# Hybrid decoder step on one core: new shares for the decode tokens' side chain

## The reference, cut to what matters

```
x += W_out( sigmoid(g_a) * P_a(SSD(xn)) + sigmoid(g_b) * P_b(DSA(xn)) ),  xn = RMSNorm(x)
x += PEER(RMSNorm(x))
```

```
ik_past = cik[page_table].reshape(bsz, past, IDX_DIM)
score = indexer_scores(iq, concatenate([ik_past, ik]), iw)      # 4097 scores per sample
_, idx = lax.top_k(score, 256)
... gather those 256 rows of cache_k and cache_v, softmax attention
```

## Time and profile before

| | us |
|---|---|
| median of 3 runs | 5932.22 (5928.28 to 5935.11) |
| the profiled execution's own time | 5921.76 |
| its span, first to last instruction | 5920.0 |
| PE busy | 4190.6 (71%) |
| DVE busy | 3636.4 (61%) |
| POOL busy | 2584.6 (44%) |
| DMA, mean over the span | 251 GB/s |

### The profile page before, as it was taken

The page is one execution under the profiler, slowest core; times in us unless marked ns, Lnnn a source line. Parts: engine busy times, 40 slices in busy tenths (PEclk is TensorE's granted clock), DMA queues, the critical chain, the costliest instruction groups (busy, mean ns, idle before and its releaser), DMA issues. The chain is left out here.

```text
span 5920.0 us, 49064 instructions
## 1 busy us (share of the span) xinstructions
PE 4190.6 (71%) x15564; PEld 2567.8 (43%) x15564; DVE 3636.4 (61%) x7802; ACT 1156.4 (20%) x2892; POOL 2584.6 (44%) x2215
## 2 busy tenths in 40 slices
PE   6956981578677887379677777668677897265666
PEld 5334871443333665153335664453333675022222
DVE  4055528766677557576766768765668556845554
ACT  2042320111322111120422221111232211011011
POOL 0000010247555444336555443246545445477776
PEclk9975995788788998689888898879788998678788
DMA  4311740569777887579889975569777889599999
GB/s 131 115 56 54 243 132 0 178 238 322 253 256 257 315 286 269 193 271 381 304 276 328 387 260 167 188 213 338 252 258 258 281 306 311 217 343 349 347 357 342
DMA packets 579367, 1484.59 MB, mean 251 GB/s; under 512 B 60088, under 2 KB 251160, under 8 KB 572600
## 3 DMA queue, kind: packets, MB, share of 16 engines
q0 software_dynamic: 307200, 1115.82, 53.6%
q1 hardware_dynamic: 258952, 331.39, 16.8%
q10 hardware_dynamic: 12960, 34.26, 1.5%
HBM read 1435.37 MB, written 45.93 MB: 250 GB/s over the span
## 5 line engine op out<-in xcount | busy, mean ns | idle before, releaser
L2640 PE MATMUL duo<-vring,diag 128*128 128x512 f32 (+1 forms) x2544 | 1403.4, 697 | 626.4 <-DMA vring<-in_peer_v,eidx 365.7
L2526 POOL DMA_INDIRECT uring<-in_peer_u,eidx x1024 | 1248.8, 1219 | 1180.9 <-DVE uring L2558 707.6
L2593 POOL DMA_INDIRECT vring<-in_peer_v,eidx x1024 | 1158.3, 1131 | 1150.9 <-PE duo L2640 540.0
L2558 DVE SCALAR_TENSOR_TENSOR uring<-uring,xr 128x1024 f32<-128x1024 f32 x1040 | 1252.7, 1221 | 268.6 <-DMA uring<-in_peer_u,eidx 224.5
L2640 PEld LDWEIGHTS duo<-vring,diag 128*128 128x128 f32 (+1 forms) x2544 | 522.7, 219 | 1364.2 <-issue 1190.5
L2673 DVE SCALAR_TENSOR_TENSOR x_tok<-vring,wt,x_tok 128x1024 f32<-128x1024 f32 x404 | 522.1, 1292 | 379.0 <-DMA vring<-in_peer_v,eidx 352.5
L637 PE MATMUL duo<-wt,xT 128*128 128x512 f32 (+3 forms) x1440 | 607.5, 581 | 89.7 <-DMA wt<-in_w_in 89.7
L637 PEld LDWEIGHTS duo<-wt,xT 128*128 128x128 f32 (+1 forms) x1440 | 241.9, 179 | 444.8 <-issue 351.7
L2621 ACT ACTIVATE diag<-ident,wt 128x128 f32<-128x128 f32 x620 | 235.3, 397 | 1011.0 <-PE duo L2640 819.5
L492 PE MATMUL duo<-xT,wx 128*128 128x264 f32 (+1 forms) x1536 | 376.7, 409 | 37.9 <-DMA wx<-in_w_in 37.7
L492 PEld LDWEIGHTS duo<-xT,wx 128*128 128x128 f32 x1536 | 311.2, 205 | 92.8 <-DMA wx<-in_w_in 38.1
(11 more groups left out here) (462 smaller groups left out, 5076.1 us busy)
## 6 DMA issues: line engine op xcount, KB each, us to landing
wt<-in_w_in SPq DMA_DIRECT2D x32, 2048.0 KB
wx<-in_w_in SPq DMA_DIRECT2D x48, 1024.0 KB
wm<-in_w_in SPq DMA_DIRECT2D x32, 1024.0 KB
wm<-in_w_branch_a SPq DMA_DIRECT2D x32, 1024.0 KB
wq<-in_peer_wq SPq DMA_DIRECT2D x32, 1024.0 KB
tokm<-tout ACTq DMA_DIRECT2D x64, 256.0 KB
eb<-decays SPq DMA_DIRECT2D x32, 512.0 KB
s_h<-in_state_ssm SPq DMA_DIRECT2D x16, 1024.0 KB
```

Source lines behind the costliest of these rows:

```text
L2526: pool.indirect_dma_start(out=E.rings.urows[K % E.ur], out_offset=None, in_=table, in_offset=bass.IndirectOffsetOnAxis(ap=E.tiles[q][3][:, ...
L2558: dve.scalar_tensor_tensor(row, row, 1.0, G.xr[:, q % 2, :], ALU.mult, ALU.mult, accum_out=G.pre[:, q % 2, j:j + 1]).then_inc(G.dotted, 1)
L2593: pool.indirect_dma_start(out=E.rings.vrows[K % E.vr], out_offset=None, in_=table, in_offset=bass.IndirectOffsetOnAxis(ap=E.tiles[q][3][:, ...
L2640: mm = pe.matmul(G.bank[6 + c][0:m, :], G.diag[:, R % DR, 0:m], E.rings.vrows[K % E.vr][:, c * BANK:(c + 1) * BANK], start=first, stop=las ...
```

## The change

The weights of job S are replaced. Their sum stays 480. The program of each engine, its instructions and their number stay as they are; only the stage in which they stand, and the place in it, differ.

```
-PLAN_SAMPLE = {"mix": 160, "norm2": 12, "pscore": 68, "route": 82, "norm1": 3, "xbc": 50, "tokproj": 105}
+PLAN_SAMPLE = {"mix": 240, "norm2": 6, "pscore": 76, "route": 48, "norm1": 0, "xbc": 40, "tokproj": 70}
```

## The result

The changed kernel is slower: 5984.02 us median (5974.69 to 5989.37) against 5930.25 us for the kernel before beside it, a ratio of 1.0093 with a 95% interval of 1.0071 to 1.0116. The forecast was 5897 us, and the measured time lies above its range of 5835 to 5970.

A forecast was written before the change was run, and what follows sets the result against it. Each stage was taken to have its own limit: TensorE in mix, VectorE in route, a TensorE sum in xbc. Stage changes of -20 and -15 us gave -35, hence 5887, or 5897 us against the median; range 5835 to 5970.

The forecast's parts named there:

- Mix, layer 0: Layer 0 mix stage: 16 entering score steps cost 48 to 61 us on nearly full TensorE; taken as +58.
- still fits, with nothing over: Layer 0 mix: an ssm sample needs 10.2 us and its slot shrinks from 12.3 to 10.7, so no charge.
- The deduction for idle time to fill: Layer 0 mix: scores fill at most 8 us of TensorE idle, so +58 was taken instead of 61.
- My sign of error: Layer 0 mix: growth by more than 65 us would mean TensorE waits for the ssm chain.
- Mix, layer 1: Layer 1 mix stage: scores cost 25 us if DMA binds, 61 if TensorE's line binds; taken as +45.
- xbc: Half 1's xbc: packing frees 65.8 us, two attend samples add 18; 133 us, -49 per layer, bounds 109 and 145.
- Rival 2: POOL's burst and DMA hold xbc at 145, layer 1's mix pays 61; 5937 us, no difference; chance 0.17.
- pscore: Scores leave pscore, search enters, clock falls to 0.82: 128 us (-5) in layer 0, 147 us (+13) in layer 1.
- my base of 76.8: Layer 1 pscore: the stage's time once the score steps have left, 76.8 us.
- the round of 2.6 us: Layer 1 pscore: a search round is 1.3 us of VectorE plus a fold of job V, 2.6 us.
- route, norm stages and tokproj: Per layer: route -4 with packing replacing search, norm1 -3, norm2 0, tokproj -17 for two samples fewer.
- The slower rival: pscore's matmuls at 1.2 GHz cost 117 us instead of 71, +46 per layer; 5989 us; chance 0.12.

The follow-up runs named there:

- the bare stage: For xbc: changed kernel with no sample work in xbc, 5961.25 us; for pscore: kernel before with only the scores moved into mix, 6004.06 us.
- the packing trial: Kernel before with search and packing all in route, attend in xbc and tokproj, scores left in pscore: 5966.6 us, ratio 1.008.

## Why the prediction was wrong

**Mix, layer 0 (+58, measured +95).** This is the step that failed. The scores' own price was nearly right: 61 forecast, 48.9 busy and 15.7 of waits measured, 64.6. Two terms were missing. I had written that the ssm part "still fits, with nothing over" and gave it nothing; TensorE waits 18.4 us for the ssm and qkv chains. The slot in that sentence was wrong: 10.7 us a sample, because I spread the added time over the whole stage, measured 9.5, which is less than the 10.2 I had worked out as needed. And I charged the lower clock in pscore alone; in mix it costs 13.4 us. The deduction for idle time to fill was wrong in sign: idle grew. The four parts make 96.4 of the 94.9. My sign of error, mix growing by more than 65 and then the ssm chain as what TensorE waits for, came true, and it names 18.4 of the 35.4 us of added idle time.

**Mix, layer 1 (+45, measured +102).** Here the choice between the bounds failed, and the bounds too. I took a value between 25 (DMA binds) and 61 (TensorE's line binds). The scores alone cost more than the upper one, 52.9 busy and 22.6 of waits; the chain waits went from 11.7 to 51.0 us, and the own matmuls grew by 9.3. Only 15 us of waits for weights were filled. That VectorE and DMA were near full told me that something would give. I read it as cover for TensorE's work, while it made the sample chain late, on which TensorE waits in order.

**xbc (-49, measured -27).** What packing frees was right: 65.8 us forecast, 182.1 - 114.0 = 68.1 measured by the bare stage. Two attend samples were priced at 18 by their share in tokproj and cost 41. I named POOL's burst and put nothing on it in the sum beyond the bounds; it is the 23.3 us wait, and spacing the gathers gives back 13 and 11. The measured 154.8 lies above the upper end of 145, and above the 150 at which I had said I would be wrong. Rival 2 had this stage's mechanism with 145 us; its price for mix was too small to carry it over the line.

**pscore (-5 and +13, measured -15 and 0).** The round count and the wait in a round were right (16 waits of 1.3). TensorE's part of a step was not: the 0.59 us of the earlier trace rows stands at 911.7, behind the barrier of 905.2 and so in route, at half the clock. In pscore a step takes TensorE 0.36 us, and in layer 0 the search costs 10.4 + 21.2 = 31.6 us and not 39. The clock was 0.86 and not 0.82 and cost about 8 us against the bare stage and not 10, and the 3 us for the last ranks were there. In layer 1 my base of 76.8 was wrong (89.0) and so was the round of 2.6 us: a fold rarely stood between. The two errors had opposite signs, so that the miss is smaller than either deserves.

**route, norm stages and tokproj** came within 4 us, though the dealing holds VectorE 9.3 us at the end of layer 0's route and not the 5 of the sum. The slower rival, a clock of 1.2 GHz in pscore, did not come: 0.86 and 0.85. By the rule of the Trainium skill (TensorE: Matmul & The Clock Gate, "HAM oscillation — how this bites in real kernels"), applied as the prediction did, pscore would have been near 174 us (the forecast's 128 and 46), and it is 117.9. That section describes waits for transfers, longer than the 1.3 us here. The trace agrees with it in part: in layer 0 the matmuls behind two waits in a row took 4.9 to 6.3 us for 3.62 at 4 of 12 points, and behind a single wait at none.

Settled: scores cost 95 and 99 us in mix and only 58 and 45 in pscore, which is the loss (+37 and +54). Moved alone they make the kernel 83 us slower, the whole change 54, so the other moves gave back some 29. Open: why route took 11 to 23 us more than the sum of its parts when it held search and packing, and how the chain waits in mix split between the shorter time and the coarse points.

## What to carry to other kernels

When due times are shares of a stage, work out the slot of each part from the points in front of it: work added behind them does not widen it. When a dependent side chain is moved into the stage where the in-order engine has the least idle time, price three things there: its busy time, the wait at each hop, and the delay of the chains that already run there and now get less of the stage. Partly idle engines are no cover for work whose every item is waited for in a queue. Before moving work between stages, move the dependent item later inside its own stage: later due times for two of TensorE's items, and for the two that follow them on ScalarE and VectorE, gave 1.0%, while the new plan cost 0.9%.

## What the runs showed that I had not expected

The granted clock follows small interruptions, and not all alike. In pscore two waits of 1.3 us or a little more in a row slowed the matmuls behind them every time, and a single one never. In layer 0's mix of the changed kernel 16 own matmuls took 3.6 to 3.7 us behind waits of 0.4 to 2.0 us, and 4.8 to 6.3 behind those of 2.2 to 3.7. So most of the clock went in the ssm and qkv part, with its waits of 3 to 4 us (0.82 from 658 to 692 us), and little in the score part (0.97 from 732 to 846). In all the own matmuls took 184.4 us instead of 171.0, with no wait above 4 us in these parts. Sixteen gathers from POOL in a row occupy its queue for 20 us, about 1.3 us each, whatever else waits in it. And the dealing of the indices by 16 small DMAs was exposed in every stage it was put in: VectorE stood 9.3 us on it in the changed route, 10.6 in the route of the packing trial, TensorE 11.1 in xbc before, and tokproj grew by 8 and 16 us when it took it over.
